# w_down of a fused decoder layer: the split operand kept in DRAM for the second column half, and nine instead of six of its 22 blocks as seven-product blocks

## The reference, cut to what matters

```python
h = rms_norm(x, ffn_norm)
return x + (jax.nn.silu(h @ w_gate) * (h @ w_up)) @ w_down   # (256 x 5632) @ (5632 x 2048)
```

## Time and profile before

| what | us |
|---|---|
| median of 3 runs (1095.08 to 1096.28) | 1096.15 |
| the profiled execution's own time | 1096.81 |
| its span | 1095.1 |
| PE busy in it | 1084.2 |
| DVE busy | 886.2 |
| ACT busy | 617.8 |
| share of the 16 DMA engines taken by SP's queue | 54.9% |

### The profile page before, as it was taken

How to read it: one execution, slowest core, us unless ns; L and a number is a source line. 1 busy time by engine, 2 the same in 40 slices (tenths; PEclk the granted TensorE clock), 3 DMA queues, 4 the chain that set the end, 5 groups by cost and what they waited for, 6 DMA issues and landing times.

```text
span 1095.1 us, 13280 instructions
## 1 busy us (share of the span) xinstructions
PE 1084.2 (99%) x5127; PEld 902.5 (82%) x5127; DVE 886.2 (81%) x822; ACT 617.8 (56%) x616; POOL 44.5 (4%) x44
## 2 busy tenths in 40 slices
PE   9999999999999999999999999999999999999997
PEld 6888889987888888888888888888888888878886
DVE  7879666754576789898898898888898898989994
ACT  7666546655755655464554555554554765555553
POOL 0077000000000000000000000000000000000000
PEclk9999999999999999999999999999999999999999
DMA  8765644654355555555555555555555655555552
GB/s 329 282 232 194 199 137 124 202 159 147 118 192 169 178 197 211 200 198 192 192 194 198 208 189 207 192 192 196 198 214 197 230 193 197 202 194 204 202 193 114
DMA packets 48550, 212.57 MB, mean 194 GB/s; under 512 B 4096, under 2 KB 9984, under 8 KB 28544
## 3 DMA queue, kind: packets, MB, share of 16 engines
q1 hardware_dynamic: 47648, 209.65, 54.9%
q10 hardware_dynamic: 864, 2.39, 0.6%
HBM read 209.93 MB, written 2.10 MB: 194 GB/s over the span
## 4 chain that ended last, share of the span: by engine, by line
PE 96%; DVE 1%; DMA 1%; ACT 1%; issue 0%; SPq 0%; DVEq 0%
PE ps L1571 73%; PE ps L1424 6%; PE ps L1426 6%; PE ps L1425 6%; PE ps L1463 2%; DMA raw<-in_w_dn 1%; PE ps L1511 1%; PE ps L1688 1%; PE ps L1689 1%; PE ps L1690 1%; PE ps L1510 0%; DMA raw<-in_w_i 0%; DVE w_lo L1296 0%; ACT t_hi L788 0%; ACT w_hi L781 0%
## 5 line engine op out<-in xcount | busy, mean ns | idle before, releaser
L1571 PE MATMUL ps<-w_hi,xp_hi 128*128 128x512 f32 x539 | 211.7, 393 | 0.0
L1571 PE MATMUL ps<-w_hi,xp_lo 128*128 128x512 f32 x539 | 210.0, 390 | 0.0
L1571 PE MATMUL ps<-w_lo,xp_hi 128*128 128x512 f32 x539 | 209.7, 389 | 0.0
L887 DVE TENSOR_TENSOR w_lo<-raw,w_hi 128x2048 fp32r<-128x2048 f32 (+2 forms) x42 | 87.3, 2078 | 85.5 <-ACT w_hi L444 85.5
L1159 DVE TENSOR_TENSOR w_lo<-raw,w_hi 128x2048 fp32r<-128x2048 f32 x55 | 125.8, 2288 | 34.4 <-ACT w_hi L692 34.4
L692 ACT ACTIVATE w_hi<-raw 128x2048 fp32r<-128x2048 f32 x55 | 105.1, 1910 | 62.1 <-DMA raw<-in_w_gu 62.1
L781 ACT ACTIVATE w_hi<-raw 128x2048 fp32r<-128x2048 f32 (+1 forms) x44 | 79.2, 1800 | 80.0 <-DMA raw<-in_w_dn 79.9
L700 ACT ACTIVATE t_hi<-t_sum 128x2048 fp32r<-128x2048 f32 x33 | 63.4, 1920 | 100.0 <-DVE t_sum L1172 100.0
L1571 PEld LDWEIGHTS ps<-w_hi,xp_lo 128*128 128x128 f32 x539 | 101.1, 188 | 21.5
L1571 PEld LDWEIGHTS ps<-w_lo,xp_hi 128*128 128x128 f32 x539 | 101.3, 188 | 20.4
L1571 PEld LDWEIGHTS ps<-w_hi,xp_hi 128*128 128x128 f32 x539 | 101.2, 188 | 20.1
(11 more groups left out here) (280 smaller groups left out, 2188.1 us busy)
## 6 DMA issues: line engine op xcount, KB each, us to landing
raw<-in_w_gu SPq DMA_DIRECT2D x88, 1024.0 KB, 4.8
raw<-in_w_dn SPq DMA_DIRECT2D x44, 1024.0 KB, 4.8
raw<-in_w_i SPq DMA_DIRECT2D x21, 1024.0 KB, 4.8
raw<-in_w_out SPq DMA_DIRECT2D x16, 1024.0 KB, 5.0
raw<-in_w_in SPq DMA_DIRECT2D x12, 1024.0 KB, 5.0
raw<-in_w_in SPq DMA_DIRECT2D x8, 576.0 KB, 3.8
raw<-in_w_i SPq DMA_DIRECT2D x6, 512.0 KB, 6.8
raw<-in_w_ukv SPq DMA_DIRECT2D x3, 1024.0 KB, 5.1
```

What stands on the lines that cost most here:

```text
L887: nc.vector.tensor_tensor(w_lo[n % 4][:, 0:k, 0:c], raw[n % 4][:, 0:k, 0:c], w_hi[n % 4][:, 0:k, 0:c].bitcast(F32), ALU.subtract).then_inc ...
L1571: mm = nc.tensor.matmul(out, x, wt, start=start and j + m == 0, stop=stop and 3 * j + m == n - 1, skip_group_check=resumed)
```

## The change

The operand of a k-pair is split once. In the first half SP stores to a DRAM buffer `xo_keep`, four blocks behind, what DVE made (and, for a seven-product block, the high part of the sums): 256 KB for a plain block, 768 KB for a seven-product block. In the second half SP loads it back, right behind the block's weights. ACT still makes the high part of the plain operand from `hid`. The ring of operand buffers grows from four to five.

The second half takes the k-pairs in a new order (`DOWN_ORDER[1]`), for which the host lays out `w_down`, and has nine seven-product blocks, at positions 0, 2, 4, up to 16, where it had six. Six of the nine reuse stored operand sums (k-pairs 0, 4, 7, 10, 13, 16). Three have k-pairs 5, 11 and 15 (positions 6, 12, 16), whose sums were not made in the first half; for these only the plain low part is loaded, and the sums are made as before. SP's loop over w_down is written out.

```diff
-DSUMS = (0, 4, 7, 10, 13, 16)
+DSUMS = ((0, 4, 7, 10, 13, 16), (0, 2, 4, 6, 8, 10, 12, 14, 16))
+DLAST = 16
+XO = 5
+DOWN_ORDER = (tuple(range(DQ)), (0, 1, 4, 2, 7, 3, 5, 6, 10, 8, 13, 9, 11, 12, 16, 14, 15, 17, 18, 19, 20, 21))
+def sums_reused(m):
+    return m >= DQ and down_sum(m) and DOWN_ORDER[1][m - DQ] in DSUMS[0]
+def xo_computed(m):
+    return m < DQ or down_sum(m) and not sums_reused(m)
+def sums_computed(m):
+    return down_sum(m) and not sums_reused(m)
...
+            def store_operand(m):
+                sp.wait_ge(xo_made, m + 1)
+                here, there = kept_blocks(m, m)
+                sp.dma_start(there, here).then_inc(xo_stored[m % XO], 16)
+            def load_operand(m):
+                q = DOWN_ORDER[1][m - DQ]
+                sp.wait_ge(xo_stored[q % XO], 16 * (q // XO + 1))
+                if m < DQ + XO:
+                    sp.wait_ge(xo_stored[m % XO], 16 * ((m - XO) // XO + 1))
+                here, there = kept_blocks(m, q)
+                sp.dma_start(here, there).then_inc(xo_in[m % XO], 16)
+            for m in range(2 * DQ):
+                load_rows(DN0 + m, (DN0 + m) % 4, w_dn[:, m:m + 1, :])
+                if 4 <= m < DQ + 4:
+                    store_operand(m - 4)
+                if m >= DQ:
+                    load_operand(m)
...
             def down_hi(m):
+                if XO <= m < DQ + XO:
+                    act.wait_ge(xo_stored[m % XO], 16 * (m // XO))
-                    act.wait_ge(xo_step, 3 * (s + 1))
-                    nc.scalar.activation(xo_hi[m % 4][:, 4:8, :], sf[:], ACT.Copy).then_inc(xo_split, 1)
+                if sums_computed(m):
+                    act.wait_ge(xo_step, 3 * (before(m, sums_computed) + 1))
+                    nc.scalar.activation(xo_hi[m % XO][:, 4:8, :], sf[:], ACT.Copy).then_inc(xo_split, 1)
...
             def down_lo(m):
+                if XO <= m < DQ + XO:
+                    dve.wait_ge(xo_stored[m % XO], 16 * (m // XO))
+                    if xo_computed(m):        # plain block: xo_lo, first half only
+                if sums_computed(m):          # the three steps of sf, and later its low part
+                if m < DQ:                    # xo_lo of a seven-product block, first half only
...
             def down_ready(m):
                 pe_.wait_ge(lo_ready, DN0 + m + 1)
-                pe_.wait_ge(xo_made, m + 1)
+                pe_.wait_ge(xo_split, m + 1 + before(m + 1, sums_computed))
+                if xo_computed(m):
+                    pe_.wait_ge(xo_made, before(m + 1, xo_computed))
+                if m >= DQ:
+                    pe_.wait_ge(xo_in[m % XO], 16 * sum(d % XO == m % XO for d in range(DQ, m + 1)))
```

More of the change, by code:

```diff
@@ L74, in in_sum, with down_sum, before @@
     return (g - 1) * NI + p // 2 if g and p < 5 and p % 2 == 0 else None
+def down_sum(m):
+    return m % DQ in DSUMS[m // DQ]
+def sums_reused(m):
+    return m >= DQ and down_sum(m) and DOWN_ORDER[1][m - DQ] in DSUMS[0]
+def before(m, counted):
+    return sum(bool(counted(d)) for d in range(m))
+def xo_computed(m):
+    return m < DQ or down_sum(m) and not sums_reused(m)
+def sums_computed(m):
+    return down_sum(m) and not sums_reused(m)
 def put(step, *units):
@@ L285, in build @@
         xo_split, xo_step, xo_made = sem("xo_split"), sem("xo_step"), sem("xo_made")
+        xo_stored, xo_in = [sem(f"xo_stored{i}") for i in range(XO)], [sem(f"xo_in{i}") for i in range(XO)]
         res_step = sem("res_step")
@@ L379, in _, with kept_blocks @@
                     load_rows(i * FB + (FF0 + p), (FF0 + p) % 4, w_gu[:, bass.ds(i * FB + p, 1), :])
-            with sp.Fori(0, HKT // 4) as i:
-                for p in range(4):
-                    load_rows(i * 4 + (DN0 + p), (DN0 + p) % 4, w_dn[:, bass.ds(i * 4 + p, 1), :])
+            def kept_blocks(m, q):
+                blocks = slice(4, 16) if q in DSUMS[0] and (m < DQ or down_sum(m)) else slice(8, 12)
+                cols = slice((blocks.start - 4) * P, (blocks.stop - 4) * P)
+                return xo[m % XO][:, blocks, :].bitcast(F32).rearrange("p a b -> p (a b)").unsqueeze(1), xo_keep[:, q:q + 1, cols]
+            def store_operand(m):
[15 more added lines that the diff above has]
+                    load_operand(m)
             for b in range(TOK):
@@ L1284, in mix_banks @@
                                         ALU.subtract if half else ALU.add).then_inc(mixed, 1)
-            def down_sums_before(m):
-                return sum(d % DQ in DSUMS for d in range(m))
             def down_lo(m):
-                n, q, slot = DN0 + m, m % DQ, (DN0 + m) % 4
+                n, q, slot = DN0 + m, DOWN_ORDER[m // DQ][m % DQ], (DN0 + m) % 4
                 x = hid[:, 2 * q:2 * q + 2, :].rearrange("p a (t c) -> p (a t) c", t=TOK)
-                if q not in DSUMS:
+                split = m + before(m, sums_computed)
+                if XO <= m < DQ + XO:
+                    dve.wait_ge(xo_stored[m % XO], 16 * (m // XO))
+                if not down_sum(m):
                     dve.wait_ge(hi_ready, n + 1)
@@ L1809, in _ @@
                 ffn(i)
-            def down_sums_before(m):
-                return sum(d % DQ in DSUMS for d in range(m))
             def down_ready(m):
                 pe_.wait_ge(lo_ready, DN0 + m + 1)
-                pe_.wait_ge(xo_made, m + 1)
+                pe_.wait_ge(xo_split, m + 1 + before(m + 1, sums_computed))
[3 more added lines that the diff above has]
+                    pe_.wait_ge(xo_in[m % XO], 16 * sum(d % XO == m % XO for d in range(DQ, m + 1)))
             def down_sums(m):
                 h, q = divmod(m, DQ)
-                slot, s, x_hi, x_lo = (DN0 + m) % 4, down_sums_before(m), xo_hi[m % 4], xo_lo[m % 4]
-                start, stop = q == 0, q == DSUMS[-1]
+                slot, s, x_hi, x_lo = (DN0 + m) % 4, before(m, down_sum), xo_hi[m % XO], xo_lo[m % XO]
+                start, stop = q == 0, q == DLAST
                 bare = {"b11": 1, "b22": 2, "b21": 3}
@@ L1850, in down_plain @@
             def down_plain(m, sides, stop=False):
[L1852 removed]
+                q, slot, x_hi, x_lo = m % DQ, (DN0 + m) % 4, xo_hi[m % XO], xo_lo[m % XO]
                 for b, up in sides:
```

81 lines of the change are left out of this document (42 added, 39 removed).

## The result

The changed kernel takes 1102.09 us (median of 5 runs, 1100.05 to 1102.79) against 1096.12 us: a ratio of 1.0054, with a 95% interval of 1.0039 to 1.0069. It is slower by 6 us where 2.2 us faster was forecast. The profiled execution took 1102.73 us, its span is 1100.8 us, 5.7 us more than before.

The account below looks back on a forecast made before the run. PE was taken as the bound, busy 1084.2 of 1095.1 us. From the profiled 1096.81 us, 2.04 (matmuls) and 0.88 (late start) gave 1093.89, taken as 1093.9 us, 0.21% under the median; range 1092.8 to 1097.0 us.

Parts of the forecast that it names:

- The matmuls: Second half of w_down: three more seven-product blocks remove 9 matmuls at 0.2267 us each, saving 2.04 us.
- the sum: Whole kernel: profiled execution's 1096.81 us less 2.04 and 0.88 us gives 1093.89 us.
- The start of the second half: Second half's first positions: shorter DVE work makes the first bank's gain timely, recovering 0.88 us of PE waiting.
- rival A: Second half's start: the late 7.2 us load was chance, so only matmuls count, 1094.1 us; chance 0.30.
- The waits in the queues, at nothing: w_down: added waits of PE, ACT, DVE and SP cost nothing, with stores taken to land in 7.0 us.
- Loads, at nothing: Second half: operand loads behind the weights cost nothing, since a heavier 340 GB/s stretch still landed weights in under 5 us.
- Stores, at nothing: First half: stores beside weight loads cost nothing, judged from 640 KB stored in 3.8 us at the trace's end.
- The bound from above, 7.2 us: Stores' effect on weights: at worst the stage's worst landing, 7.2 us instead of 4.8.
- The rule of the Trainium skill: DMA landings: HBM access takes 0.2 us on average, 2 us at high load, so landings grow by up to 1.8 us.
- Rival C: First half: stores make weights late and seven-product blocks stall, 1097.5 us, or 1098.4 with longer landings; chance 0.08 at full price.
- Rival B: Second half, position 2: late gains or ACT's t_hi use up 0.2 us of room, 1094.7 to about 1095 us; chance 0.12.
- Rival D: SP's queue: slow stores make its wait delay next weights by 1 to 3 us, 1095 to 1097; 0.08 with smaller C.

Follow-up runs that it names:

- loads only: Changed kernel without its stores except k-pair 0's; all 22 second-half loads stay and read that one block: 1093.86 us, ratio 0.9977.
- that with six: Changed kernel with stores and loads only for the six k-pairs whose sums are used again, 768 KB each: 1097.54 us, ratio 1.0018.
- the run with one store: Kernel before plus a single 768 KB store, of k-pair 13, behind the weights of position 17; nothing loaded back: 1098.04 us, ratio 1.0018.
- stores only: Kernel before with the changed kernel's 22 stores added and nothing loaded back: 1103.74 us, ratio 1.0068.
- small stores: Kernel before with 22 stores added, all of 256 KB, and nothing loaded back: 1100.90 us in one run.
- the run without DRAM: Changed kernel's nine seven-product blocks and new order, without any store or load, all operands computed anew: 1106.04 us, ratio 1.0094.

## Why the prediction was wrong

**The matmuls (2.04 us): right.** 5118 matmuls, the same distance; with loads only the profiled execution took 1094.08 us where the sum said 1093.89.

**The start of the second half (0.88 us): right for the profiled execution.** PE does not wait for gains there any more. But rival A was right about the median: the late load comes and goes. In the three runs with a single store, whose second half is that of the kernel before, the weights in question landed in 4.7, 4.9 and 6.9 us. The 1093.86 us of loads only are 2.5 us under the median beside it, by the interval 1.4 to 3.6 us, which can't tell 2.04 from 2.92.

**The waits in the queues, at nothing: right to within 0.3 us,** which is what the sum for the stage leaves over. SP waits 2.0 us in all for stores to land, and no next load of weights is due then. ACT's and DVE's waits for stored buffers and PE's extra waits do not show, although stores took up to 10.3 us to land where 7.0 was assumed.

**Loads, at nothing: right where they run without stores.** In the changed kernel from 1005 to 1073 us the weights land in 4.9 us at 274 GB/s; with loads only PE never waits, though one landing takes 7.3 us. Two exceptions: where the last stores and the first loads meet, weights landed in up to 8.1 us, and the third stop (0.5 us) starts there; and a 768 KB load in the place of the store before the mixing cost PE 1.47 us.

**Stores, at nothing: this step failed.** The prediction said that no row shows stores beside loads and then took "nothing, since the 3.8 us are in line with loads of that size". That row was of a queue with nothing else in it. Measured: one 768 KB store puts 1.5 us on the weights issued just before it and 2.8 us on the next; 22 stores put 3.9 us (8.7 instead of 4.8) on the median of the weights issued between 897 and 930 us. The bound from above, 7.2 us, was too low too, since it came from a stage without stores; the landings went to 9.3 us. The rule of the Trainium skill that was weighed there, "DMA: Bandwidth & Descriptors", section "Latency and other measured facts", would by the prediction's estimate have added up to 1.8 us. The trace agrees with its sign where there are stores, not where there are loads alone, and measured about twice its size.

**Rival C: the mechanism, but not its place and price.** It had stores make the weights of the first half late, at a chance of 0.08 for the full price. Three things were missed. First the place: C looked at seven-product blocks alone, and of its five only the one at position 13 cost PE more than 0.1 us (2.0 us). The prediction asked about the mixing only in the second half. In the first half DVE has the whole mixing behind `w_lo` of position 18. The weights of position 18 were issued at 934.46, 15.3 us before PE needed the mixed banks, and landing, ACT's high part, DVE's low parts and the mixing take all of that but 0.56 us. DVE's last step of the mixing that PE waits for, and PE's first matmul of position 18, before the change:

```profile
947.97 1.23 DVE L1283 TENSOR_TENSOR ps<-ps,mix 128x1024 f32<-128x1024 f32 x1
...
949.76 0.39 PE L1571 MATMUL ps<-w_hi,xo_hi 128*128 128x512 f32 x1
```

Mixed at 949.20, wanted at 949.76. Shown: one store costs 1.9 us there and 0.2 us, no more than noise, six positions earlier. Second, the delays add up: C delayed single loads, while from position 11 to 16 the weights of every block, plain or not, land in 8.2 to 9.3 us, so that DVE starts the seven-product block at position 13 behind late plain ones. Third, the clock: 3.4 of the 9.0 us are matmuls at half speed behind the two long stops.

**Rival B** (a wait at position 2 of the second half) did not come. **Rival D** (the queue is held) neither.

**Why a store takes more than a load** of its size is not settled. Shown are the direction (6.3 us between stores and loads of equal size and place), that it is not the row distance in DRAM, that one small store is free, and that stores on another queue, at other times, still leave a part of the delay.

## What to carry to other kernels

A transfer that the trace does not show (here a store amid a full stream of loads) must be priced by its effect on the stream beside it; its own time in an empty queue says little. Before traffic is added, look up for every load in that stretch what stands behind its consumer in the in-order queue: the room to ask for is that of the tightest thing behind it, not that of the block itself. And sums of work over a stage say too little where long and short pieces alternate; count the longest run of long ones.

## What the runs showed of the hardware

A 768 KB store beside 1 MB loads delays not only the next load (7.6 instead of 4.8 us) but also the one issued 0.4 us before it (6.3 us), in the runs with one store as in that with six. A 768 KB load at such places, from position 8 on, leaves the one before it at 4.7 to 5.0 us and the next at 4.8 to 6.9. A 256 KB store alone adds 0.5 us, then nothing.

After the stops of 2.0 and 3.2 us PE ran at a granted clock of 0.57 and 0.56 for 4 us, at 1.7 us a time, as much as half the stop again or more. After the stop of 2.3 us in the run with one store it did not, granted clock 1.00 from 952.6 to 957 us:

```profile
952.60:957.00 4.40, 4.34 (x19) 3.61 (x20) 4.37 (x3) 1.78 (x1) 0.00 (x0) 1.00 0.44 186
```

So the length of the stop alone does not tell whether the clock falls. In other traces it fell behind stops of 2.8 us (stores only) and 3.0 us (small stores), and did not behind the eight stops of 1.1 to 1.9 us of the run without DRAM. What made it fall behind 2.0 us and not behind 2.3 stays open.
